# State-space outputs of a decoder kernel: two products against four, with a sum on VectorE

## The reference

```python
bu_re = jnp.einsum('blgc,gnc->blgn', ug, bb_re)
bu_im = jnp.einsum('blgc,gnc->blgn', ug, bb_im)
x_re, x_im = jax.vmap(_scan_one, in_axes=(None, None, 0, 0))(
    jnp.broadcast_to(a_re, shp), jnp.broadcast_to(a_im, shp), bu_re, bu_im)
y = (jnp.einsum('blgn,gcn->blgc', x_re, c_re.astype(jnp.float32))
     - jnp.einsum('blgn,gcn->blgc', x_im, c_im.astype(jnp.float32)))
y = y + d_skip.astype(jnp.float32).reshape(SSM_GROUPS, SSM_GROUP) * ug
y = jax.nn.gelu(y.reshape(B_, L, SSM_WIDTH).astype(h.dtype))
y = y * jax.nn.sigmoid(y @ w_glu + b_glu)
return (y * jax.nn.silu(z)) @ w_out
```

## Time and profile before

| | before |
|---|---|
| time, median of 3 runs | 3204.83 us (3203.48 to 3205.46) |
| the profiled execution: its time, its span | 3204.72 us, 3202.9 us |
| TensorE matmul busy | 3122.3 us (97%) |
| VectorE busy | 1764.5 us (55%) |
| ScalarE busy | 480.6 us (15%) |
| GpSimd (POOL) busy | 294.2 us (9%) |
| chain that ended last | TensorE 93%, DMA 3%, VectorE 2% |
| mean granted TensorE clock | 0.993 |

### The profile page before, as it was taken

How to read it: one execution, slowest core, us unless ns; L and a number is a source line. 1 busy time by engine, 2 the same in 40 slices (tenths; PEclk the granted TensorE clock), 3 DMA queues, 4 the chain that set the end, 5 groups by cost and what they waited for, 6 DMA issues and landing times.

```text
span 3202.9 us, 55954 instructions
## 1 busy us (share of the span) xinstructions
PE 3122.3 (97%) x23706; PEld 2875.6 (90%) x23706; DVE 1764.5 (55%) x2703; ACT 480.6 (15%) x944; POOL 294.2 (9%) x153
## 2 busy tenths in 40 slices
PE   5999999989999999999999999999999999999999
PEld 3788888878889988898888888899999999999999
DVE  6348844544145455575536844667665555555443
ACT  2204510010001233312300012220000000000000
POOL 0004310000000555220000000000010000000000
PEclk8999999999999999999999999999999999999999
DMA  9874468766573423244344342424544444444443
GB/s 408 342 294 159 193 251 324 292 267 251 234 291 136 155 106 132 106 158 158 118 174 151 150 145 106 140 95 163 188 165 167 161 179 157 176 164 171 161 164 134
DMA packets 51027, 599.51 MB, mean 187 GB/s; under 512 B 9535, under 2 KB 12190, under 8 KB 13342
## 3 DMA queue, kind: packets, MB, share of 16 engines
q1 hardware_dynamic: 50846, 596.88, 48.5%
HBM read 593.70 MB, written 3.16 MB: 186 GB/s over the span
## 4 chain that ended last, share of the span: by engine, by line
PE 93%; DMA 3%; DVE 2%; ACT 1%; DVEq 1%; POOLq 1%; issue 0%; POOL 0%; SPq 0%; ACTq 0%
PE bank L2686 25%; PE bank L796 21%; PE bank L286 17%; PE bank L745 11%; PE bank L316 4%; PE bank L742 2%; PE bank L328 2%; DMA ring<-in_t_mod 2%; PE bank L567 1%; PE aux L1681 1%; PE bank L394 1%; PE bank L557 1%; DMA ring<-in_t_u 1%; PE aux L1728 1%; PE aux L1258 1%; PE bank L1276 1%
## 5 line engine op out<-in xcount | busy, mean ns | idle before, releaser
L796 PE MATMUL bank<-hT,ring 128*128 128x128 f32 x3776 | 459.5, 277 | 1.1 <-POOLq L1666 1.0
L796 PEld LDWEIGHTS bank<-hT,ring 128*128 128x128 f32 x3776 | 439.9, 192 | 15.8 <-issue 13.7
L2686 PE MATMUL bank<-arena,ring 128*128 128x128 f32 x3440 | 396.4, 275 | 0.0
L2686 PEld LDWEIGHTS bank<-arena,ring 128*128 128x128 f32 x3440 | 390.2, 192 | 0.0
L286 PE MATMUL bank<-arena,ring 128*128 128x256 f32 x1536 | 336.4, 381 | 7.4 <-ACT arena L1021 5.0
L286 PEld LDWEIGHTS bank<-arena,ring 128*128 128x128 f32 x1536 | 292.3, 191 | 47.9 <-issue 5.7
L745 PE MATMUL bank<-hT,ring 128*128 128x256 f32 x1472 | 321.8, 380 | 0.0
L745 PEld LDWEIGHTS bank<-hT,ring 128*128 128x128 f32 x1472 | 278.4, 190 | 39.6 <-issue 2.5
L286 PE MATMUL bank<-hT,ring 128*128 128x256 f32 x1024 | 226.0, 383 | 2.9 <-DMA ring<-in_t_u 2.9
L286 PEld LDWEIGHTS bank<-hT,ring 128*128 128x128 f32 x1024 | 196.1, 192 | 30.2 <-issue 3.2
L796 PE MATMUL bank<-arena,ring 128*128 128x128 f32 x1728 | 207.8, 275 | 1.5 <-DVEq L607 1.5
(11 more groups left out here) (449 smaller groups left out, 3982.6 us busy)
## 6 DMA issues: line engine op xcount, KB each, us to landing
ring<-in_t_mod SPq DMA_DIRECT2D x64, 2048.0 KB, 13.3
ring<-in_t_gu SPq DMA_DIRECT2D x44, 2048.0 KB, 7.5
ring<-in_t_out SPq DMA_DIRECT2D x16, 2048.0 KB, 7.6
ring<-in_t_zs SPq DMA_DIRECT2D x16, 2048.0 KB, 7.5
ring<-in_t_down SPq DMA_DIRECT2D x16, 2048.0 KB, 7.3
ring<-in_t_gdn SPq DMA_DIRECT2D x12, 2048.0 KB, 7.6
ring<-in_t_u SPq DMA_DIRECT2D x8, 2048.0 KB, 9.8
ring<-in_t_z SPq DMA_DIRECT2D x8, 2048.0 KB, 9.7
```

The lines of the kernel that those rows point to most:

```text
L796: last = nc.tensor.matmul(out[:, P * at:P * at + P], a[:, j, :], tile_at(b, j), start=j == 0 and q in (0, 3), stop=j == half - 1 and q in ...
L2686: last = nc.tensor.matmul(out[:, P * q:P * q + P], a[:, j, :], b[:, j, :], start=begins and q == 0 and j == 0, stop=ends and q == len(grou ...
```

## The change

Ahead of the outputs of a block VectorE adds `ZS` onto `ZC`, so that the two planes of `ZC` are real and imaginary part themselves, and TensorE multiplies each with its matrix: two products in place of four. For that POOL writes its product with the planes exchanged, as two instructions of 128x512 instead of one of 128x1024. The sum of block b - 1 is made in VectorE's iteration b behind the turning of the inputs and ahead of the scans; the last one stands behind the loop. TensorE waits for the new signal `summed` instead of `turned` and `z_sined`. POOL no longer waits for `y_ready`. The new semaphore takes the place of one that wasn't used.

```diff
@@ -186,7 +186,7 @@
         sel_ready = sem("sel_ready")
         rows_ready_m = sem("rows_ready_m")
         cols_ready = sem("cols_ready")
-        mod_ready = sem("mod_ready")
+        summed = sem("summed")
         sq_ready = sem("sq_ready")
         ms_ready = sem("ms_ready")
         std_ready = sem("std_ready")
@@ -1261,23 +1261,22 @@
 
             def outputs(b):
 
-                pe.wait_ge(turned, b + 1)
-                pe.wait_ge(z_sined, b + 1)
+                pe.wait_ge(summed, b + 1)
                 if b:
                     pe.wait_ge(ysum_ready, b)
                 y = bank[2][:, 0:T]
-                zc, zs = planes(ZC), planes(ZS)
+                z = planes(ZC)
                 for k in range(4):
                     rows = slice(32 * k, 32 * k + 32)
                     nc.tensor.matmul(y[rows, 0:P], K0[rows, 32 * b:32 * b + 32], u_all[rows, b, 0:P], start=True, stop=False)
-                for m, (c, z, r) in enumerate(((CA_RE, zc, 0), (CA_RE, zs, 1), (CA_IM, zs, 0), (CA_IM, zc, 1))):
+                for r, c in enumerate((CA_RE, CA_IM)):
                     for k in range(4):
                         rows, at = slice(32 * k, 32 * k + 32), 32 * (4 * b + k)
-                        nc.tensor.matmul(y[rows, 1:P], c[:, at:at + 32], z[:, k, r, 0:P - 1], start=False, stop=m == 3)
-                for m, (c, z, r) in enumerate(((C_RE, zc, 0), (C_RE, zs, 1), (C_IM, zs, 0), (C_IM, zc, 1))):
+                        nc.tensor.matmul(y[rows, 1:P], c[:, at:at + 32], z[:, k, r, 0:P - 1], start=False, stop=r == 1)
+                for r, c in enumerate((C_RE, C_IM)):
                     for k in range(4):
                         rows, at = slice(32 * k, 32 * k + 32), 32 * (4 * b + k)
-                        last = nc.tensor.matmul(y[rows, P:2 * P], c[:, at:at + 32], z[:, k, r, :], start=m == 0, stop=m == 3)
+                        last = nc.tensor.matmul(y[rows, P:2 * P], c[:, at:at + 32], z[:, k, r, :], start=r == 0, stop=r == 1)
                 last.then_inc(y_ready, 1)
 
             wait_drained(pe, "u")
@@ -1317,6 +1316,12 @@
                 v.scalar_tensor_tensor(u_all[:, b, :], u_all[:, b, :], col("ssm_d", b, 1), bank[2][:, 0:T],
                                        ALU.mult, ALU.add).then_inc(ysum_ready, 1)
 
+            def turned_sum(b):
+
+                dve.wait_ge(z_sined, b + 1)
+                v.tensor_tensor(ZC, ZC, ZS, ALU.add)
+                dve.drain().then_inc(summed, 1)
+
             v.nop().then_inc(bu_used, 1)
             dve_turns(dve, 1)
             for b in range(SBLOCKS):
@@ -1334,7 +1339,10 @@
                 dve.drain()
                 v.tensor_tensor(z[:, :, 0, :], z[:, :, 0, :], ms[:, :, 1, :], ALU.subtract)
                 v.tensor_tensor(z[:, :, 1, :], z[:, :, 1, :], ms[:, :, 0, :], ALU.add)
-                dve.drain()
+                if b:
+                    turned_sum(b - 1)
+                else:
+                    dve.drain()
                 for k in range(4):
                     m = mag2[:, 4 * b + k:4 * b + k + 1].to_broadcast([P, P])
                     for r in range(2):
@@ -1348,6 +1356,7 @@
                 v.tensor_tensor(zc[:, :, 0, :], z[:, :, 0, :], co3, ALU.mult)
                 v.scalar_tensor_tensor(zc[:, :, 1, :], z[:, :, 1, :], -1.0, co3, ALU.mult, ALU.mult)
                 dve.drain().then_inc(turned, 1)
+            turned_sum(SBLOCKS - 1)
             finish(SBLOCKS - 1)
 
         def dve_z_bias(dve):
@@ -1383,9 +1392,9 @@
                     turns_of(b + 2)
 
                 pool.wait_ge(turned, b + 1)
-                if b:
-                    pool.wait_ge(y_ready, b)
-                g.tensor_tensor(planes(ZS), planes(Z[b % 2]), both(NSIN[b % 2]), ALU.mult)
+                z, zs, si = planes(Z[b % 2]), planes(ZS), NSIN[b % 2].rearrange("p (k n) -> p k n", k=4)
+                for r in range(2):
+                    g.tensor_tensor(zs[:, :, 1 - r, :], z[:, :, r, :], si, ALU.mult)
                 pool.drain().then_inc(z_sined, 1)
 
         def act_glu(act):
```

## The result

The changed kernel takes 3209.68 us (median of 20 runs, 3206.61 to 3211.17), the kernel before 3203.76 in as many (one of these took 4049.47 and is left out of the ratio). The ratio is 1.0018, with a 95% interval of 1.0012 to 1.0024: 5.9 us slower (3.8 to 7.7). The ratio itself lies inside the 0.2% that was called no change, its interval reaches a little past it. Half of the products of the state-space outputs are gone and the time isn't lower.

The account below looks back on a forecast made before the run. TensorE bounds the stage before; then a loop through VectorE's sum, TensorE, ScalarE's copy and the angles, 23.70 us per two blocks against 23.07. The stage ends 3.2 later: 3204.72 + 3.2 = 3207.9, forecast 3208.0 us, own range 3205 to 3211, overall 3203.0 to 3214.5.

Parts of the forecast that it names:

- What bounds the stage: State-space stage: TensorE bounds it before; afterwards a loop through sum, copy and angles, 23.70 us per two blocks against 23.07.
- a pair: Two successive blocks of the state-space stage, odd and even; forecast to take 23.70 us, against 23.07 before.
- Its terms: Pieces of the odd block's loop: 5.04 to the outputs, 1.35 outputs, 1.10 inputs, 7.10 dense piece, 0.05, then 9.06 us.
- S + 5.04: Earliest start of the previous block's outputs, 5.04 us after VectorE begins a block (S); before it was 3.54.
- What else moves: Scans meet a POOL instruction in odd blocks; even block starts 11.3 us after the odd; stalls 1.75 and 0.62.
- The sum over the stage: Added up over the blocks, the next stage begins at 420.02 instead of 416.81, 3.2 us later.
- The cover holds: Rival: in the state-space stage TensorE stays the bound, so the kernel gets 14.0 us faster, 3190.8; chance 0.09.
- if everything else still arrived in time: Condition on the gain from removed state-space matmuls: two blocks would then take 21.33 us, 1.74 less.
- VectorE is held by POOL: Rival: state-space VectorE instructions with two SBUF inputs wait beside POOL, 0.7 us per two blocks, 3212.9; chance 0.12.
- The clock falls in the stalls: Rival: TensorE's clock drops after state-space stalls, 1.2 us lost seven times, 3216.4; chance 0.07.
- the row at 461 of before: Profile row at 461 us: clock stayed at 1.00 after 1.93 us idle; used as evidence against clock falls.

Follow-up runs that it names:

- e8: Changed kernel with ScalarE's copies of the finished dense product and the modulation's row moved behind the next block's angles; 3204.35 us, ratio 1.0000.
- e6: Changed kernel with TensorE doing the next block's inputs ahead of the previous block's outputs; 3203.55 us, ratio 0.9999.
- e2: Changed kernel with four products again; VectorE still makes the sum, into a room nobody reads, and TensorE doesn't wait for it; 3204.34 us, ratio 1.0002.
- e11: Changed kernel with three useless matmuls ahead of the outputs in each even block, to fill TensorE's stall; 3208.91 us, ratio 1.0016.
- e1: Changed kernel without the sum and its wait, two products kept, so the sine products are left out of the output; 3194.45 us, ratio 0.9971.
- e5: Changed kernel with the sum moved ahead of the two subtractions of the turning; 3209.95 us, ratio 1.0014.
- e7: e6 with four of the 16 dense matmuls of a block also moved ahead of the outputs; 3203.87 us, ratio 0.9999.
- e9: e7 with the angles' first product made by ScalarE in four instructions instead of by POOL; 3197.39 us, ratio 0.9981.
- e4: Changed kernel run again without edits, for a second profile; 3209.59 us, ratio 1.0017 to the kernel before.
- e12: Changed kernel run again without edits, for a third profile; 3209.76 us, ratio 1.0020 to the kernel before.

## Why the prediction was right, and where it was not

- *What bounds the stage.* Right: the loop VectorE, sum, TensorE, ScalarE's copy, angles, VectorE. Worked out 23.70 a pair, measured 23.70; with four products 24.57 and 24.57. e8, which takes the copy out of the loop, e6, which shortens the part behind the sum, and e2, which has the work and not the wait, leave no room for VectorE's throughput.
- *Its terms.* The sum 1.22 as taken. Outputs at S + 5.04; L1271 starts at 289.29, S + 4.97, on the timeline, where before's started at 288.76 and the chain, from which the forecast was read, had 288.83, so it is the same. POOL's halves 2.51 (2.5), and L1340 unhindered (0.69). L1240 at S + 14.64 (14.64), then 9.07 (9.06).
- *What else moves.* The scans' meeting with L1377 was foreseen: 3.43. The even block starts 11.47 after the odd (11.3), the stalls are 0.40 and 1.82 (0.62 and 1.75).
- *The sum over the stage.* + 3.2 forecast, + 3.34 in the profile of after. The median of the runs is 5.9 over, at the upper part of the forecast's own range (3205 to 3211). **The rest, about 2.5 us, isn't settled.** 0.3 of it lies outside the core's span (2.1 us around it, 1.8 in before). A fall of the clock in the stage, seen in two profiles of three, costs 1.1 where it counts, but e11 has none and is still 5.4 over before. What moves single executions of after is seen in its three profiles, of 3208.1, 3210.6 and 3206.3 us. Block 1 begins at 236.94, 238.47 and 236.82, so up to 1.6 us apart before the first sum; the second has the fall at 350; and what follows the stage takes 2787.8, 2787.6 and 2786.0 us. There TensorE waits for the glu weights near 460, and behind that wait the clock fell in the first two, for 3 to 4 us, and not in the third. The profile of before has the late beginning (238.84) and no such fall (2786.1 us behind the stage), that of e6 has none either, and all the others have one. How often either happens in the timed runs of the two kernels, no trace shows, and e1 and e2 have that fall without being slower than their loops say. The loop accounts for 3.3 of the 5.9 us; the rest stands in no term of the forecast, and that the range was wide enough for it is in part luck.
- *The cover holds.* Fell, as forecast. But its price was wrong: it took all 13.9 us of the removed matmuls as the gain (3190.8), and e1 shows 9.2 (3194.45). The step that failed is the one that said "if everything else still arrived in time": POOL's product with the sine is next in line and costs TensorE 2.9 us of waiting, and the loop of VectorE, POOL and ScalarE without TensorE (10.73 a block in e1, 21.46 a pair) was not worked out beside TensorE's 21.33. Another 1.3 are the clock at the beginning of the stage, which has nothing to do with the change.
- *VectorE is held by POOL.* Not at the sum, which costs its 1.22, nor at L1340. But the meeting itself, of an instruction with two SBUF inputs with one of POOL, lengthens the blocks of e5 and e7, where VectorE is last, and e9 takes 5.3 us off e7 by removing it. The Trainium skill (GPSIMD Engine Reference, section 8, Key points) names just this meeting; the traces agree (3.43 with POOL beside it, 2.63 without).
- *The clock falls in the stalls.* Given 0.07, and it happens, though not in each stall: twice in three profiles with 19 idle times of 1.8 in all (7, 6 and 6 in the stage), behind all four of 2.0 to 2.1 in e5, and never in e6, e8 and e11, where none is above 1.53 but one of 1.83 in e8. My price for one, 1.2 a pair, was near (1.14 and 0.85). What I had wrong was that it either happens in all of seven pairs or in none. The Trainium skill's warning about short idles between groups of matmuls (TensorE: Matmul & The Clock Gate, the section on a second HAM failure mode) agrees with the four falls of e5 and the two of after, and not with e6 and e8, whose stalls of 1.4 and 1.5 in every pair brought none; the row at 461 of before had spoken against it too strongly.

## What to carry to other kernels

A saving on the busiest engine is worth only as much as the next loop allows, so write out that loop, with every engine that it passes through, before counting the instructions saved. When a new wait is put in front of an engine with a fixed order, charge it to whoever waits for the work queued behind it; and move work that doesn't need the new result ahead of the wait, and what delays others (here a copy) away from the end of the queue. An edit off the bound shows nothing until the bound has moved: try it again then, as the angles on ScalarE.

## What the runs showed of the hardware

- Eight scans of 128x128 take 2.63 us alone and 3.43 beside a POOL product of 1.05, so the meeting costs VectorE 0.8 us, three quarters of what POOL needs.
- TensorE's granted clock fell behind 2 of 19 idle times of 1.8 us in the three profiles of after, and behind 4 of 4 of 2.0 to 2.1 in e5. The length alone doesn't decide it: behind the wait for the glu weights it fell after 2.15 us (after) and 1.99 (e4), and not after 2.13 (e6), 2.19 (e12) and 1.93 (before). It stayed down for some 3 to 4 us each time.
- Two POOL products of 128x512 in a row take 2.51 us, one of 128x1024 2.37, so the same work in two instructions takes 0.14 us more.
